# Two weight slots and the memory loaded a stage ahead, and one layer's memory keys and values computed at another's norm: a two-block model on one core of Trainium2

## What is computed

```python
# end of the first block
x = x + gt_f[:, None, :] * moe(h, ...)
x = rms_norm(x, g_final)
# the two layers, i = 0 and 1
h = x @ a_w_in if i == 0 else x @ b_w_in
...
mem_out = memory_cross_attention(q_mem, mem, w_mem_kv[i])    # kv = mem @ w_kv, 256 memory rows
sub = jnp.concatenate([mix, mem_out], axis=-1) @ w_mix_out[i]
x = layer_norm(ALPHA * x + sub, ln_mix_g[i], ln_mix_b[i])
x = layer_norm(ALPHA * x + swiglu(x, w_ffn_in[i], w_ffn_out[i]), ln_ffn_g[i], ln_ffn_b[i])
```

## Time and profile before

| | us |
|---|---|
| median of 3 runs | 2024.46 (2019.44 to 2028.82) |
| the profiled execution, its time | 2020.84 |
| the profiled execution, its span | 2019.0 |
| TensorE busy | 1853.7 |
| VectorE busy | 754.2 |
| ScalarE busy | 552.2 |
| mean granted TensorE clock, of full speed | 0.968 |

### The profile page before, as it was taken

The page is one execution under the profiler, slowest core; times in us unless marked ns, Lnnn a source line. Parts: engine busy times, 40 slices in busy tenths (PEclk is TensorE's granted clock), DMA queues, the critical chain, the costliest instruction groups (busy, mean ns, idle before and its releaser), DMA issues. The chain is left out here.

```text
span 2019.0 us, 25094 instructions
## 1 busy us (share of the span) xinstructions
PE 1853.7 (92%) x10306; PEld 1214.2 (60%) x10306; DVE 754.2 (37%) x1091; ACT 552.2 (27%) x811; POOL 11.7 (1%) x23
## 2 busy tenths in 40 slices
PE   7999998779999999999999999978899997989998
PEld 6799876643333332333333333328789987869996
DVE  5767644431111111111111111106565555655555
ACT  3444554210000000000000000005544434534442
POOL 0000000000000000000000000000000000000000
PEclk9999999779999999999999999989999998989999
DMA  9877642299999999999999999968345546325552
GB/s 332 311 258 237 235 138 74 96 372 429 431 431 432 431 431 432 431 432 431 431 431 431 431 431 431 431 261 285 125 146 177 180 146 208 117 92 167 188 172 100
DMA packets 152474, 592.99 MB, mean 294 GB/s; under 512 B 7603, under 2 KB 82527, under 8 KB 127824
## 3 DMA queue, kind: packets, MB, share of 16 engines
q1 hardware_dynamic: 150176, 583.90, 73.1%
q0 software_dynamic: 2224, 8.04, 1.2%
HBM read 590.84 MB, written 1.07 MB: 293 GB/s over the span
## 5 line engine op out<-in xcount | busy, mean ns | idle before, releaser
L1426 PE MATMUL psum<-expert_ring,expert_arena 128*64 128x512 f32 x2048 | 453.9, 597 | 21.3 <-DMA expert_ring<-in_w_mlp_dram 21.3
L1426 PEld LDWEIGHTS psum<-expert_ring,expert_arena 128*64 128x64 f32 x2048 | 142.2, 137 | 316.8 <-issue 272.6
L320 DVE TENSOR_TENSOR layer_w_lo<-layer_ring,layer_w_hi 128x1024 fp32r<-128x1024 f32 x190 | 231.4, 1224 | 242.3 <-ACT layer_w_hi L315 242.1
L315 ACT CAST layer_w_hi<-layer_ring 128x1024 fp32r<-128x1024 f32 x190 | 197.6, 1047 | 243.6 <-PE psum L365 123.5
L363 PE MATMUL psum<-layer_x_hi,layer_w_hi 128*128 128x256 f32 x864 | 249.9, 289 | 13.2 <-DVE layer_w_lo L320 10.2
L1442 PE MATMUL psum<-expert_ring,expert_arena 128*64 128x512 f32 x1024 | 234.0, 601 | 30.1 <-DMA expert_ring<-in_w_mlp_dram 29.2
L364 PE MATMUL psum<-layer_x_lo,layer_w_hi 128*128 128x256 f32 x864 | 248.7, 288 | 0.0
L365 PE MATMUL psum<-layer_x_hi,layer_w_lo 128*128 128x256 f32 x864 | 248.5, 288 | 0.0
L1314 DVE TENSOR_SCALAR expert_arena<-psum 128x512 f32<-128x512 f32 x32 | 22.1, 692 | 557.0 <-PE psum L1426 557.0
L363 PEld LDWEIGHTS psum<-layer_x_hi,layer_w_hi 128*128 128x128 f32 x864 | 170.4, 197 | 15.6 <-issue 11.8
L1442 PEld LDWEIGHTS psum<-expert_ring,expert_arena 128*64 128x64 f32 x1024 | 68.7, 137 | 176.1 <-issue 117.8
(11 more groups left out here) (271 smaller groups left out, 1983.9 us busy)
## 6 DMA issues: line engine op xcount, KB each, us to landing
expert_ring<-in_w_mlp_dram SPq DMA_DIRECT2D x192, 2048.0 KB, 23.3
layer_ring<-in_w_ffn_in_dram SPq DMA_DIRECT2D x44, 1024.0 KB, 5.0
mixer_ring<-in_w_in_dram SPq DMA_DIRECT2D x38, 1024.0 KB, 6.8
mixer_ring<-in_w_ada_dram SPq DMA_DIRECT2D x24, 1024.0 KB, 5.9
layer_ring<-in_w_ffn_out_dram SPq DMA_DIRECT2D x20, 1024.0 KB, 4.9
layer_ring<-in_b_w_in_dram SPq DMA_DIRECT2D x10, 1024.0 KB, 7.3
layer_ring<-in_w_mix_out_dram SPq DMA_DIRECT2D x8, 1024.0 KB, 5.0
layer_ring<-in_a_w_in_dram SPq DMA_DIRECT2D x7, 1024.0 KB, 9.2
```

The lines of the kernel that those rows point to most:

```text
L315: self.nc.scalar.copy(hi, raw).then_inc(self.hi_ready, 1)
L320: self.nc.vector.tensor_tensor(lo, raw, hi.bitcast(FP32), ALU.subtract).then_inc(self.lo_ready, 1)
L1426: last = nc.tensor.matmul(U[CAP * h:CAP * h + CAP, N * n:N * n + N], xg[:, k, j, :], ring[:, at:at + N], start=False, stop=k == KC - 1)
```

## The change

Layer 0's first two slots (km0's and vm0's) and the memory are loaded by SyncE in the expert block, behind its last load; the memory goes to `base`, the slots to a tile of their own, `slots_ahead`, which outlives the stages and whose memory held the experts' transposed rows (`actT`, needed only until the router's `lg1`). Layer 1's first two slots (qm's and q_0's) are loaded by SyncE at the end of layer 0. `slots_ahead` is the first half of each layer's ring, and the ring of its own keeps two slots. `g_final` is loaded by GpSimd instead of SyncE. km1 and vm1 leave the head of layer 0 and stand around `yT` at its first norm: km1 ahead of it, vm1 behind. There three units are split ahead of the update of pr1's tile 1, not one (`ahead=3`). The sums move from job km0 to the third split, the final norm from vm0 to km0. The copy of km1's and vm1's result on ScalarE, the 96 matmuls, and all other work are as they were.

```diff
@@ -247,7 +248,8 @@
-                    before, after = job.units[shared:shared + 1], job.units[shared + 1:]
...
+                    before, after = job.units[shared:shared + job.ahead], job.units[shared + job.ahead:]
             for u in (*later, *before) if job.units else before:
@@ -282,6 +286,10 @@
+    def slot(self, q):
+        ring, at = self.ring[q % self.ring_slots]
+        return ring[:, at:at + SLOT]
@@ -1055,7 +1061,7 @@
     arena = ctx.enter_context(nc.sbuf_tensor("expert_arena", [P, 10752], FP32))
-    actT = ctx.enter_context(nc.sbuf_tensor("expert_hT", [P, KC, S], FP32))
+    actT = free(M["ahead"], 0, KC, S)
@@ -1180,6 +1186,13 @@
+            wait_freed(sp, "lg1")
+            sp.wait_ge(h_ready, T)
+            sp.dma_start(free(M["base"], 0, T, D), A["mem_2"][0].rearrange("(t p) d -> p t d", p=P)).then_inc(M["mem_here"], 16)
+            for n, src in enumerate(first_slots(A, 0)):
+                load_ahead(sp, M, 0, n, src)
             further_rounds(sp, one_round, second_flag(sp))
@@ -1504,6 +1517,17 @@
+def first_slots(A, i):
...
+    w, wide, rows = (A["b_w_in_2"][0], 3 * W_MIX, 0) if i else (A["w_mem_kv_2"][0], 0, W_MEM)
+    return [w[:, at:at + WIDE].rearrange("(k p) n -> p k n", p=P) for at in (wide, rows)]
...
+def load_ahead(sp, M, i, n, src):
+    dst = M["ahead"][:, SLOT * n:SLOT * n + SLOT].rearrange("p (k n) -> p k n", n=WIDE)
+    sp.dma_start(dst, src).then_inc(M["ahead_here"][i][n], 16)
@@ -1514,7 +1538,7 @@
     arena = ctx.enter_context(nc.sbuf_tensor(f"layer{i}_arena", [P, 9728], FP32))
-    ring = ctx.enter_context(nc.sbuf_tensor(f"layer{i}_ring", [P, RING_LAYER * SLOT], FP32))
+    ring = ctx.enter_context(nc.sbuf_tensor(f"layer{i}_ring", [P, (RING_LAYER - 2) * SLOT], FP32))
     high = ctx.enter_context(nc.sbuf_tensor(f"layer{i}_w_hi", [P, BUFFERS, UNIT], F32R))
@@ -1524,7 +1548,7 @@
     u_nat, wsT, v_nat, v_rows = free(arena, 0, T, W_MIX), free(arena, 1536, HEADS, P), free(arena, 3072, T, W_MIX), free(arena, 4608, 2, W_MIX)
-    mem_nat = free(arena, 0, T, D)
+    mem_nat = free(M["base"], 0, T, D)
     qT, kT, v_self = free(arena, 0, QK, S), free(arena, 1536, QK, S), free(arena, 3072, T, W_MIX)
@@ -1564,9 +1588,8 @@
         transposes("memT")
-        for n in range(DEPTH_2):
-            jobs.add(f"km{n}", "act", jobs.wide(w_kv[n], 0))
-            jobs.pair(f"vm{n}", "act", jobs.rows(w_kv[n], W_MEM, W_MEM))
+        jobs.add("km0", "act", jobs.wide(w_kv[0], 0))
+        jobs.pair("vm0", "act", jobs.rows(w_kv[0], W_MEM, W_MEM))
         jobs.banks, jobs.turn = list(range(BANKS)), 0
@@ -1615,8 +1638,14 @@
     for half in range(2):
-        jobs.pair(f"pr{half}", "dve", jobs.rows(A["w_mix_out_2"][i], N * half), apart=half == 1)
-    transposes("yT")
+        jobs.pair(f"pr{half}", "dve", jobs.rows(A["w_mix_out_2"][i], N * half), apart=half == 1, ahead=1 if i else 3)
+    if i == 0:
...
+        jobs.add("km1", "act", jobs.wide(w_kv[1], 0))
+        transposes("yT")
+        jobs.pair("vm1", "act", jobs.rows(w_kv[1], W_MEM, W_MEM))
+    else:
+        transposes("yT")
     w_ffn = A["w_ffn_in_2"][i]
@@ -1628,12 +1657,13 @@
-        stream = Stream(nc, sem, jobs, ring, RING_LAYER, high, low)
+        slots = [(M["ahead"], 0), (M["ahead"], SLOT), (ring, 0), (ring, SLOT)]
+        stream = Stream(nc, sem, jobs, slots, RING_LAYER, high, low, M["ahead_here"][i])
         full, freed_by_act, freed_by_dve, wait_freed = stream.full, stream.freed["act"], stream.freed["dve"], stream.wait_freed
...
             sem("fin_here"), sem("sums_taken"), sem("squares_ready"), sem("mean_ready"), sem("fin_root_ready"), sem("fin_ready"))
-        rows_here, mem_here, ws_here, v_rows_here, bs_here = sem("rows_here"), sem("mem_here"), sem("ws_here"), sem("v_rows_here"), sem("bs_here")
+        rows_here, mem_here, ws_here, v_rows_here, bs_here = sem("rows_here"), M["mem_here"], sem("ws_here"), sem("v_rows_here"), sem("bs_here")
         step_sem, var_ready, root_ready, v_ready, x_sums_ready = sem("dve_step"), sem("var_ready"), sem("root_ready"), sem("v_ready"), sem("x_sums_ready")
@@ -1656,13 +1686,16 @@
             if i == 0:
-                sp.dma_start(mem_nat, A["mem_2"][0].rearrange("(t p) d -> p t d", p=P)).then_inc(mem_here, 16)
                 sp.dma_start(bs, A["a_b_s_2"][0]).then_inc(bs_here, 16)
-            for q in range(len(jobs.slots)):
+            for q in range(stream.loaded, len(jobs.slots)):
                 stream.load(sp, q)
-                if i == 0 and q == 1:
-                    sp.dma_start(g_fin.unsqueeze(1), A["g_final"].rearrange("(o d) -> o d", o=1).partition_broadcast(P)).then_inc(fin_here, 16)
-            if out is not None:
+            if out is None:
...
+                for n, src in enumerate(first_slots(A, i + 1)):
+                    old = max(q for q in range(len(jobs.slots)) if q % RING_LAYER == n)
+                    sp.wait_ge(stream.lo_ready, jobs.slots[old][2][-1] + 1)
+                    load_ahead(sp, M, i + 1, n, src)
+            else:
                 for t in range(T):
@@ -1671,12 +1704,15 @@
             if i == 0:
+                pool.dma_start(g_fin.unsqueeze(1), A["g_final"].rearrange("(o d) -> o d", o=1).partition_broadcast(P)).then_inc(fin_here, 16)
                 for n, name in enumerate(("a_ln_v_g_2", "a_ln_v_b_2")):
...
+                pool.wait_ge(full, jobs.full("memT11"))
             for n, name in enumerate(("ln_mix_g_2", "ln_mix_b_2", "ln_ffn_g_2", "ln_ffn_b_2")):
@@ -1703,7 +1739,7 @@
                 pair = b.rearrange("p (a s) -> p a s", a=2)
-                if name == "vm0t0" and i == 0:
+                if name == "km0":
                     final_roots()
@@ -1825,13 +1861,13 @@
                 if what == "split":
+                    if job == 2 and i == 0:
+                        take_sums()
                     stream.split_low(dve, job)
...
                 if name == "km0":
-                    take_sums()
-                if name == "vm0t1":
                     final_norm()
@@ -2052,7 +2088,10 @@
         mixer(nc, M, A, scratch)
+        M["mem_here"] = ctx.enter_context(nc.semaphore("mem_here"))
+        M["ahead_here"] = [[ctx.enter_context(nc.semaphore(f"ahead_here{i}{n}")) for n in range(2)] for i in range(DEPTH_2)]
         M["later"] = sb("later_consts", [P, TABLE_W["later"]])
+        M["ahead"] = sb("slots_ahead", [P, 2 * SLOT])
         M["kv"] = sb("memory_kv", [P, DEPTH_2 * 1024])
```

More of the change, by code:

```diff
@@ L180, in add, with pair @@
         return job
[L182 removed]
+    def pair(self, name, by, slots, apart=False, ahead=1):
         for t in range(T):
[L187 removed]
+            job = self.add(f"{name}t{t}", by, slots)
+            job.apart, job.ahead = apart, ahead
     def piece(self, name, by, slots):
@@ L262, with __init__ @@
 class Stream:
-    def __init__(self, nc, sem, jobs, ring, ring_slots, high, low):
+    def __init__(self, nc, sem, jobs, ring, ring_slots, high, low, here=()):
         self.nc, self.jobs, self.ring, self.ring_slots, self.high, self.low = nc, jobs, ring, ring_slots, high, low
@@ L561, in sem @@
             return ctx.enter_context(nc.semaphore("mix_" + name))
-        stream = Stream(nc, sem, jobs, ring, RING_MIX, high, low)
+        stream = Stream(nc, sem, jobs, [(ring, SLOT * n) for n in range(RING_MIX)], RING_MIX, high, low)
         full, freed_by_act, freed_by_dve = stream.full, stream.freed["act"], stream.freed["dve"]
```

15 lines of the change are left out of this document (6 added, 9 removed).

## The result

The changed kernel took 2002.98 us (median of 4 runs, 2000.96 to 2004.29), the kernel before 2023.69 beside it (4 runs): a ratio of 0.9892, 95% interval 0.9876 to 0.9908. This ratio is an estimate from the runs and not the quotient of the two medians, which is 0.9898. The forecast was a gain of 13.9 us and a median of 2010.6, in a range of 2002 to 2019; the difference of these medians is 20.7, and the measured time lies 1 us above the lower end of that range. The change was measured twice more, with 0.9909 (0.9895 to 0.9923) and 0.9919 (0.9905 to 0.9932), so the three ratios put its gain at 16 to 22 us. The profiled execution took 2000.96, with a span of 1998.7 against 2019.0.

What follows compares the result with a forecast made beforehand. TensorE, busy 92%, was taken as the bound, with time to win only at its stands or low clock outside the weight-bound expert block. Head −14.4, first norm +4.8, layer 1 −4.3 gave −13.9 us: 2010.6 us, range 2002 to 2019.

Steps and rivals of the forecast that it cites:

- Loads ahead cost nothing: Expert block's end: three 1 MB loads on SyncE behind the last expert load land near 1350, ahead of 1353.8, at no cost.
- Step 1: Head of layer 0: the memory's transposes begin at 1354.0, 0.2 us after the block's first DMA, an estimate.
- Step 2: Head of layer 0: km0 begins at 1360.5, takes 8.24 us to 1368.7, the sums just hidden; vm0 ends at 1374.5.
- Step 3: Head of layer 0: the final norm becomes the chain to watch; x ready at 1375.2 and 1376.4, allowing vn0 at 1380.6.
- Step 4: Head of layer 0: ws lands at 1380.4 after a 2.9 us stand; vn0 at 1382.0, 1383.5 in effect; gain 14.4 us.
- 1.5 us of low level behind that stand: Head of layer 0: 1.5 us added for low clock behind the ws stand, between 0 and km0's 2.5.
- First norm, +4.8: First norm: 96 matmuls, 11.5 us of work, added behind the projection cost 4.8 us; bounds 3.8 and 7.5.
- Layer 1, −4.3: Head of layer 1: slots loaded ahead remove ScalarE's 0.83 us and the stand before q_0; gain 4.3 us, bounds 2.7, 5.5.
- Sharing with the last expert load: Rival, expert block's end: loads ahead share engines with that load, delaying it up to 7 us; −7, 2017.5; chance 0.08.
- A late ws: Rival, head of layer 0: ws or the final norm comes later than reckoned, costing 5; −9, 2015.5; chance 0.13.
- Loads that do not arrive: Rival, head of layer 0: loads ahead land after the block's start, TensorE still stands for them; −8, 2016.5; chance 0.04.
- TensorE at the low level through the head: Rival, head of layer 0: three stands keep TensorE's clock low, a loss of 12.5 us, 2037; chance 0.04.

Runs made afterwards that it cites:

- e1: The kernel before with only the loads ahead (g_final on GpSimd's queue); km1, vm1, sums and final norm at their old places: 2011.43 us, 0.9938.
- e2: The kernel before with only km1 and vm1 moved to the first norm, sums and final norm moved too, no loads ahead: 2017.37 us, 0.9963.
- e3: The change, but layer 1 loads its first two slots itself, not ahead: 2010.66 us, 0.9932 of the kernel before.
- e4: The change with one weight split, not three, ahead of tile 1's norm update at the first norm: 2009.0 us, 0.9935 of the kernel before.
- e6: The kernel before with three idle 1 MB loads behind the last expert load, into used slots that nothing reads: 2022.38 us, 1.0002.
- a0_again: The change measured again without any edit: 2004.95 us, 0.9909 of the kernel before.
- v1: The change with ws loaded at the layer's start and x's low parts made ahead of two weight units': 2000.51 us, 0.9901 of the kernel before.
- e5: The change with ws loaded by GpSimd at the layer's start and the squares placed elsewhere: 2005.34 us, 0.9917 of the kernel before.
- v2: v1 with each layer's first two weight units split ahead of the casts of what is transposed: 2001.88 us, 0.9903 of the kernel before.

## Why the prediction was right and wrong

The direction, the three places and the sign of each were right, and e1 to e4 show the mechanism of each. The size was short by nearly 30%: 13.9 us forecast, 19.3 to 19.8 by the traces.

The step that failed is the fourth of the head. It let ws alone hold vn0, with a stand of 2.9 us and 1.5 us of low level behind it, which put vn0 in effect at 30.3 us after the zeros matmuls. The runs showed vn0 at 26.8 to 27.2 in the three executions of the change: a stand of 2.2 to 2.7 us, no low level behind it, and a second chain, the low parts of x, that ends 0.2 to 0.7 us ahead of the transposes of ws. The second term that failed is the stretch from vn0 to the end of pr1, which the sum leaves out, and so puts at nothing, without a reason; it gave 1.4 us. Point by point, counted from the end of the zeros matmuls (1353.23 before):

- *Loads ahead cost nothing*: right for the last expert load, by e6; some tenths of a us may be lost in the gap ahead of the zeros matmuls. They landed near 1349 in the change and between 1351 and 1352 in a0_again (there the GB/s fall), some 3.5 us ahead of the layer's start.
- *Step 1, the memory's transposes 0.8 us later*: 0.6.
- *Step 2, km0 begins at +7.3*: +7.1, and the sums of the experts were hidden, as said. But *km0 takes 8.24 us* was wrong: 7.6 in all three executions of the change. Its matmuls start 0.21 us apart until 1363.03 and 0.12 apart from then on, so the low part lasted 3.7 us. It was priced as before, where it lasted 5.5. In e1 and v1, with the same loads ahead, it lasted 5.7 and 5.5 again, so this too varies from execution to execution.
- *Step 3, x scaled by +22.0*: +21.0; 0.7 of the difference is km0.
- *Step 4, ws lands 7.9 us after its issue and vn0 begins at +28.8*: it landed in 6.9 us and vn0 began at +27.1. In the kernels that load it at this place 6.9 to 8.7 us were seen. The stand was 2.2 us, not 2.9. The Trainium skill's formula (DMA: Bandwidth & Descriptors, section "Anatomy of one DMA — SWDGE (gpsimd) path") gave an estimate of 3.8 us, and no run came near it. At the layer's start (e5, v1, v2) the same load took even 11.7. The prediction named ws as the only thing ahead of vn0. It was not: e5 took it away and gained 0.1 to 0.4 us, since the low parts of x were as late.
- *1.5 us of low level behind that stand*: this is the largest single miss of the head. The stretch behind it shows 1.00. In e3 (0.74) and e5 (0.66) the level did fall at that place, so the term is real in some executions and absent in all three of the change.
- *Nothing between vn0 and pr1's end*: −1.4. TensorE has the same stands there in all kernels, the longest of 3.25 and 2.45 us, both for ScalarE. The granted clock falls behind both of them in five executions (before, e1, e5, e6, v2), and this column has 83.1 or more there; it falls behind only one of them in the seven others, of which six have 81.6 to 81.8 and e3, low behind ws too, 82.5. (e5 and e6 ran low at a third place too.) So one fall more costs some 1.4 us. A stretch that the change doesn't touch was taken as fixed; over the twelve executions it varies from 81.6 to 86.2. All three kernels that keep km1 at the head (before, e1, e6) are among the five. Whether the move has a part in it or chance alone is not shown.
- *First norm, +4.8*: +6.2 up to fg0 (6.3 forecast), −1.7 behind it for the restart that is now at the high level (1.5 forecast), in all: +4.5. This is the best of the terms. It rested on three splits being ahead of tile 1's norm, which e4 shows.
- *Layer 1, −4.3*: −4.9; −0.9 of it up to qm, as said.

Sum of what was missed: head 3.2 (0.7 km0, 1.0 ws, 1.5 clock), between 1.4, norm 0.3, layer 1 0.6: 5.5 us. About half of it, 2.9 us, is the granted clock at two places where it differs between executions, so that part of the gain is luck as far as these runs show. The forecast median was 7.6 us too high. Of that, 5.9 are the profiled execution (2006.9 against 2000.96), in which layer 0 also started 1 us earlier than in the one before; the other 1.6 are that the median lay 2.0 us above the profiled execution and not 3.6, as assumed from three runs.

Of the rivals, none came true. Sharing with the last expert load: excluded by e6. A late ws: its landing reached 8.7 us once, in e3, and never 13.2. Loads that do not arrive: none. TensorE at the low level through the head: no, the level came back inside km0 in every kernel here.

## What to carry to other kernels

- Waits for loads at a stage's start can be removed by issuing its first loads at the tail of the queue of the stage ahead, behind the last load that is needed there: here the landing of that one did not move. The gain is the DMA wait alone (6.7 and 4.1 us here), for the splits behind it remain.
- Independent work moved into a stand pays for the stand and for the low clock behind it, provided that what it needs is ready when the stand begins. Here two splits more in front of a norm were covered, and leaving them out cost 4.2 us.
- When a stand names one releaser, look up when the second one is done before pricing its removal. Here it was 0.3 us behind, and removing the first gave 0.1 to 0.4 us instead of 2.2.
